# A hybrid encoder layer on eight cores: the transposes move from the matmul engine to DMA transposes on one queue

## The reference, cut to what matters

```python
def layer(x, c, S0, conv_prev, p):
    mod = (c @ w_mod + b_mod)[:, None, :]
    sh1, sc1, g1, sh2, sc2, g2 = jnp.split(mod, N_MOD, axis=-1)
    h = rmsnorm(x, norm1_g) * (1 + sc1) + sh1
    m, S_new, buf = token_mixer(h, S0, conv_prev, ...)
    x = x + g1 * m
    h = rmsnorm(x, norm2_g) * (1 + sc2) + sh2
    gt, upv = jnp.split(h @ w_ffn_in, 2, axis=-1)
    x = x + g2 * ((jax.nn.silu(gt) * upv) @ w_ffn_out)
    return x, S_new, buf

def token_mixer(h, S0, conv_prev, ...):
    q, k, v, g, a, cb, cc, ch, ga, gb = split(h @ w_in)      # D_MODEL 1024, IN_DIM 8208
    S_new, o = gla_recurrence(q, k, v, log_sigmoid(a @ w_alpha + b_alpha) / 16, S0)
    o = rmsnorm per head(o) * gla_norm_g * silu(g)
    y_a = o @ w_gla_out
    conv, new_buf = causal_conv(cc * ch, conv_prev, conv_w, conv_b)
    y_b = (cb * conv) @ w_conv_out
    return (sigmoid(ga) * y_a + sigmoid(gb) * y_b) @ w_o, S_new, new_buf
```

## Time and profile before

| | |
|---|---|
| median of 3 runs | 1441.21 us (1440.6 to 1496.53) |
| the profiled execution | 1442.98 us, span of its slowest core 1441.4 us (others 1428.5 to 1437.5) |
| mean granted TensorE clock | 0.969 to 0.979 |
| PE, DVE, ACT busy | 92%, 48%, 35% of the span |
| chain that ended last | 74% on PE |

### The profile page before, as it was taken

How to read it: one execution, slowest core, us unless ns; L and a number is a source line. 1 busy time by engine, 2 the same in 40 slices (tenths; PEclk the granted TensorE clock), 3 DMA queues, 4 the chain that set the end, 5 groups by cost and what they waited for, 6 DMA issues and landing times.

```text
span 1441.4 us, 22660 instructions; the slowest of 8 cores (1428.5 to 1441.4 us)
## 1 busy us (share of the span) xinstructions
PE 1333.1 (92%) x7660; PEld 695.5 (48%) x7660; DVE 688.4 (48%) x1257; ACT 504.3 (35%) x1122; POOL 109.8 (8%) x208
## 2 busy tenths in 40 slices
PE   1577999998989899889999999999999999999997
PEld 1333445444545455544445555555555445555443
DVE  1467557543656577642233334962122552212486
ACT  1576456432445455431211112981111001111233
POOL 3000100000000000011110120010000002000000
PEclk9778999998999999999999999999999999999999
DMA  9736401206211111154342366532223006222222
GB/s 173 212 117 154 52 9 30 52 2 59 51 23 23 23 23 23 23 96 73 52 74 38 62 102 135 179 68 37 40 35 44 1 1 103 36 40 35 59 103 110
DMA packets 42797, 92.66 MB, mean 64 GB/s; under 512 B 5206, under 2 KB 8166, under 8 KB 42684
## 3 DMA queue, kind: packets, MB, share of 16 engines
q0 software_dynamic: 29264, 53.02, 24.9%
q1 hardware_dynamic: 13420, 38.20, 8.2%
HBM read 133.95 MB, written 10.25 MB: 100 GB/s over the span
## 4 chain that ended last, share of the span: by engine, by line
PE 74%; ACT 9%; DMA 5%; DVE 5%; issue 5%; POOL 0%; ACTq 0%; DVEq 0%; SPq 0%; POOLq 0%
PE psum L464 72%; ACT sb_arena L447 6%; DMA sb_wring<-wfm 2%; DVE sb_arena L450 2%; PE psum L467 2%; ACT sb_tmpB L447 2%; DMA sb_wring<-w_in 1%; ACT sb_rstd L447 1%; DMA sb_wring<-w_mod 1%; DVE sb_arena L454 1%; DVE sb_arena L458 1%; DMA sb_arena<-xm 1%; DVE sb_tmpB L458 0%; POOL sb_wring L437 0%; DVE sb_arena L455 0%
## 5 line engine op out<-in xcount | busy, mean ns | idle before, releaser
L464 PE MATMUL psum<-sb_arena,sb_wring 128*128 128x384 bf16 (+3 forms) x4448 | 837.5, 347 | 11.5 <-DVE sb_arena L461 10.1
L464 PEld LDWEIGHTS psum<-sb_arena,sb_wring 128*128 128x128 bf16 x4448 | 430.1, 98 | 385.3 <-issue 44.2
L464 PE MATMUL psum<-sb_wring,sb_arena 128*128 128x512 bf16 (+2 forms) x1596 | 350.4, 378 | 4.3 <-DMA sb_wring<-w_in 4.3
L447 ACT ACTIVATE sb_tmpB<-psum 128x384 f32<-128x384 f32 (+1 forms) x264 | 139.6, 532 | 606.3 <-PE psum L464 576.1
L450 DVE TENSOR_TENSOR sb_arena<-psum,sb_tmpB 128x384 bf16<-128x384 f32 (+5 forms) x254 | 148.6, 587 | 324.6 <-PE psum L464 306.1
L464 PEld LDWEIGHTS psum<-sb_wring,sb_arena 128*128 128x128 bf16 (+1 forms) x1596 | 155.8, 99 | 184.0 <-issue 7.4
L437 POOL DMA_DIRECT2D sb_wring<-wfm x140 | 75.3, 545 | 912.5 <-PE psum L464 769.0
L450 DVE TENSOR_TENSOR sb_tmpB<-psum,sb_tmpB 128x384 f32<-128x384 f32 (+2 forms) x80 | 47.8, 598 | 171.0 <-PE psum L464 170.5
L450 DVE TENSOR_TENSOR sb_arena<-psum,sb_arena 128x512 f32<-128x512 f32 (+2 forms) x106 | 72.6, 685 | 35.3 <-PE psum L464 35.1
L447 ACT ACTIVATE sb_arena<-sb_arena 128x1024 bf16<-128x1024 f32 (+2 forms) x60 | 60.5, 1010 | 76.7 <-DVE sb_arena L450 61.8
L467 PE MATMUL psum<-sb_identb,sb_arena 128*128 128x128 bf16 (+2 forms) x636 | 58.4, 234 | 24.6 <-DVE sb_arena L454 22.1
(11 more groups left out here) (94 smaller groups left out, 582.3 us busy)
## 6 DMA issues: line engine op xcount, KB each, us to landing
sb_wring<-wfm POOLq DMA_DIRECT2D x140, 256.0 KB, 6.1
sb_arena<-xm SPq DMA_DIRECT2D x29, 512.0 KB, 5.5
sb_arena<-xp SPq DMA_DIRECT2D x16, 512.0 KB, 8.2
ym<-sb_arena SPq DMA_DIRECT2D x16, 512.0 KB, 2.7
sb_wring<-w_ffn_out POOLq DMA_DIRECT2D x22, 256.0 KB, 4.6
sb_wring<-w_in POOLq DMA_DIRECT2D x16, 256.0 KB, 9.7
sb_wring<-w_mod POOLq DMA_DIRECT2D x16, 256.0 KB, 7.8
sb_wring<-w_o POOLq DMA_DIRECT2D x8, 256.0 KB, 8.0
```

What stands on the lines that cost most here:

```text
L447: return P.op("act", lambda e: e.activation(out=out, in_=in_, func=func, **kw), reads=reads, writes=writes)
L464: return P.op("pe", lambda e: e.matmul(out, lhsT=lhsT, rhs=rhs, start=start, stop=stop), reads=reads, writes=writes)
```

## The change

Every transpose of rows (`norm_b`, `post`), of the recurrence's output (`gla_C`) and of the prefix keys (`pre_ktm`) becomes a DMA transpose issued by SP, SBUF to SBUF in bf16. The 600 PE transposes of these places go; 124 others stay. One DMA transpose takes a whole tile of 128 rows by 1024 features (33 tiles in the prelude, 17 in the recurrence, 17 in the output projection); the four of the keys take 128 by 2048. The result arrives unmodulated in its final place, and DVE modulates it there in place, 8 operations of up to 512 columns a block, where ACT and DVE shared this work before. In `wo_gen` the scaling of the rows moves from DVE to ACT. Row loads move from SP to POOL, except those of the first two blocks; the residual rows are loaded by POOL behind the weights of `w_o`, with the first two feed-forward weights among them. The first two prefix blocks are normed (and block 1 is loaded) ahead of `mod_fm_gen`; the load of block 1 waited for the twelfth weight before. The prelude's rounds are arranged anew, the fillers in `wo_gen` are five in place of two, the first two feed-forward tiles take the last group last, and the last `taps` of a convolution channel runs a step earlier.

```diff
-        for c_ in (1536, 512, 1024):
+        hTp, r_hTp, r_hTpr = [], [], []
+        for c_ in (0, 512, 1024, 1536):
...
+        def dmat(out, in_, reads, writes):
+
+            return P.op("sp", lambda e: e.dma_start_transpose(out=out, in_=in_), reads=reads, writes=writes, dma=True)
...
-                dma("sp", xin[xi][0:R, :], src, after, [r_xin[xi]])
+                dma("sp" if i < 2 else "pool", xin[xi][0:R, :], src, after, [r_xin[xi]])
...
+                if i < NPB:
+                    dmat(hTp[i % 4][:, :, j * 128:(j + 1) * 128], xnP[xo], [r_xnP[xo]], [r_hTpr[i % 4][j]])
+                else:
+                    t = GTILES[i - NPB][j]
+                    dmat(hT[:, :, t * 128:t * 128 + R], xnP[xo][0:R, :], [r_xnP[xo]], [r_hTr[t]])
...
+            for k in range(KT):
+                for (c, n, seq) in runs:
+                    v = dst[:, k, col0 + c:col0 + c + n]
+                    ts(v, v, modT[:, 1, k, seq:seq + 1], modT[:, 0, k, seq:seq + 1], ALU.mult, ALU.add, raws + [r_modT[1], r_modT[0]], [dregs[k]])
+                if k % 2 == 1:
+                    yield
...
         def pre_ktm(pb):
+
             st = pb % 2
-            for t in range(4):
-                ki = pb * 4 + t
-                b = newbank()
-                for h in range(NH):
-                    tr(psb(b)[:, h * 128:(h + 1) * 128], kdP[st][:, h, t * 128:(t + 1) * 128], identb[:, :], [r_kdP[st][h], r_identb], [r_ps[b]])
-                cp(kdtmP[ki], psb(b)[:, 0:512], [r_ps[b]], [r_kdtmP[ki]])
-                yield
+            dmat(kdtmP[pb].rearrange("p (a d) -> p a d", a=16), kdP[st].rearrange("p h t -> p (h t)"), r_kdP[st], [r_kdtmP[pb]])
...
-            bT = mbank()
-            for k in range(KT):
-                tr(psb(bT)[:, k * 128:k * 128 + R], ogb[oi][0:R, k * 128:(k + 1) * 128], identb[0:R, 0:R], [r_ogb[oi], r_identb], [r_ps[bT]])
-            cp(ogT[:, :, c0:c0 + R], psb(bT).rearrange("p (k r) -> p k r", k=KT)[:, :, 0:R], [r_ps[bT]], [r_og[t]])
+            dmat(ogT[:, :, c0:c0 + R], ogb[oi][0:R, :], [r_ogb[oi]], [r_og[t]])
...
-                    cx, r_cx = taps(g)
-                    yield
-                    cv(g, cx, r_cx)
+                    tp = taps(g)
                     if g == 3:
-                        cx, r_cx = taps(4)
+                        tp4 = taps(4)
+                    yield
+                    cv(g, *tp)
                     yield
-                cv(4, cx, r_cx)
+                cv(4, *tp4)
...
+                act(xv[xi][0:R, :], xres[0:R, t, :], AF.Copy, r_xres[t] + [r_rstd[gi]], [xg[xi]], scale=rstd[0:R, gi * 4:gi * 4 + 1])
+                dmat(h2T[:, :, c0:c0 + R], xv[xi][0:R, :], [xg[xi]], [r_h2r[t]])
...
+                if t in (8, 11, 14, 17, 18):
                     next(filler)
...
+                for g in range(NG):
+                    if t == min(GTILES[g][-1] + 3, 18):
+                        post(g)
...
+                order = [(j, g) for j in range(2) for g in range(NG - 1)] + [(0, NG - 1), (1, NG - 1)] + order[2 * NG:]
...
+        begin(1)
+        run(nas[1])
+        run(mod_fm_gen([(0, 0, 0), (1, 1, 1)]))
...
-        ldafter = [[mdregs[11]]]
-        begin(1)
         begin(2)
         run(norm_t(0))
...
+        begin(3)
+        spread([(pre_gate(0), 6), (norm_t(1), 4)])
         state = pre_state()
+        spread([(nas[2], 7), (pre_gate(1), 6), (pre_keys(0, wk), 4)])
+        pre_ktm(0)
         for s_ in range(0, NBK - 2):
 
             parts = []
-            begin(s_ + 3)
             begin(s_ + 4)
+            parts.append((chain(iter([None] * 2), norm_t(s_ + 2), iter([None] * 2)), 8))
...
+            kb = s_ + 1 if s_ == 0 else s_
+            if kb < NPB and s_ != 1:
+                parts.append((pre_keys(kb, wk), 4))
+            if 1 <= s_ < NPB - 1:
                 parts.append((pre_gate(s_ + 1), 6))
...
+            dma("pool", xres[0:R, t, :], x_src(t), [], r_xres[t])
+            if t == 5:
+                f1w[0] = (wfm("f1", 0), wfm("f1", 22))
```

More of the change, by code:

```diff
@@ L28 @@
 TM = 2112
-TX = 2114
+TX = 2128
 GRP = [(0, 512), (512, 384), (896, 384), (1280, 384), (1664, 448)]
@@ L268, in build, with raw_regs @@
         r_hTh = mreg("hTh", [(A0 + (k * TX + TM) * 2, A0 + (k * TX + TX) * 2) for k in range(KT)], "hT")
+        def raw_regs(name, off, width, cols, grp_):
+            return [mreg("%s_%d" % (name, i), [(off + (k * width + c0) * 2, off + (k * width + c0 + n) * 2) for k in range(KT)], grp_)
+                    for i, (c0, n) in enumerate(cols)]
+        r_hTr = raw_regs("hTr", A0, TX, CH, "hTr")
         xres = view(A0, 17 * 4096, F32).rearrange("p (n d) -> p n d", d=D)
@@ L284, in build @@
         r_h2 = fm_regs("h2", B0, KT, TM, GRP, "h2")
+        r_h2r = raw_regs("h2r", B0, TM, CH, "h2r")
         nfg = view(B0, 4096, F32)
```

127 lines of the change are left out of this document (47 added, 80 removed).

## The result

The changed kernel takes 1521.1 us, the kernel before 1441.0 us beside it on the same chip: 1.055 times as long, 95% interval 1.053 to 1.057. It is 5% slower where 3% faster was forecast. In some executions the cores of one die run at a lower clock (1626 and 1696 us here, 1497 before); the ratio leaves these out and the median does not, and by the ratio the loss is 78.7 us. The profiled core's span went from 1441.4 to 1516.6 us, 75 us more.

A forecast was written before the change was run, and what follows sets the result against it. PE, busy 92% of the span, was taken as the bound except where it waits. Prelude and start 22, recurrence 13 and output projection 7 made 42 us off the 1441.4 us span, for 1400 us; range 1370 to 1430.

The forecast's parts named there:

- 1 to 2 us a piece for the queue: Prelude: a 256 KB DMA transpose occupies the queue 1 to 2 us and lands after 2 to 3 us.
- The start, "+5": Start: loading block 1 wholly beside the weights PE waits for costs 5 us, between nothing and 11.6.
- first gate matmul later than 50 us: Start of the prelude: sign that the forecast is wrong, for the first gate matmul behind `mod_fm_gen`.
- 1.3 us in each of seven rounds: Prelude: DVE's exposed wait for a block's four transposes, 9 us in all.
- the queue rival: Prelude and output projection: transposes run one after another and limit the pace; at 6.1 us each, 1560 us; chance 0.12.
- 0.71 of the sum: Prelude, 42 to 160 us: same overlap of PE and ACT work afterwards, 85 us, 33 less; 36 with later transposes.
- the named 0.7: Prelude: a clock below 0.7 was a sign that the forecast is wrong.
- the rival's 0.5: Prelude: mean clock falls from 0.80 to 0.5 as PE idles more, eating the gain; 1421 us, chance 0.18.
- The recurrence, 13 us: Recurrence: 7.5 us of transposes, 4 of waits at channel heads and 1.5 of clock saved; between 7.5 and 19.
- The output projection, 7 us off: Output projection: 17 tiles fall from 3.96 to 3.54 us each, limited by DVE; 1.5 us with dearer modulations.
- 0.28 us a modulation: Output projection: DVE's price for modulating 384 columns, from an SBUF row; 0.40 by the PSUM row.
- The eight-fold price: Prelude and output projection: eight pieces of 1.31 us a tile, 10.5 us a tile, about 1796 us; chance 0.03.

The follow-up runs named there:

- e4: Changed kernel with squares, scaling and transposes of block 1 written behind the modulation vectors' matmuls; 1518.4 us.
- e10: e9 with row loads of blocks 0 and 1 first, then modulation vectors, then scaling and transposes of both blocks; 1482.6 us.
- e9: Changed kernel with row loads of each block held, by a bare dependence, until the transposes two blocks earlier have landed; 1486.8 us.
- e13: e10 with the next stage's weight loads held until the last prelude block's transposes have landed; 1474.4 us.
- e14: e13 with the modulation of a block moved to the end of its round; 1473.2 us.
- e1: Kernel before with only the recurrence's part of the change (output tiles by DMA transpose, earlier taps); 1431.3 us, ratio 0.993.
- e17: e1 with five 512 KB copies through GpSimd's queue beside each output tile, its transpose held until the first has landed; 1538.7 us.

## Why the prediction was wrong

The forecast span was 1399.4 us and the measured 1516.6, 117 us more: 89 of them lie ahead of `ss`, 3 in the recurrence, 27 in the output projection, and 2 go the other way elsewhere. The step that failed most is the price of a transpose, "1 to 2 us a piece for the queue", taken from a quiet row and used beside loads. There it was up to 13 us.

- **The start, "+5".** It was 29 us. I priced block 1's load as bytes beside the weights (2.1 MB), and did not follow the order on SP: the load is issued behind four transposes, which took 31 us beside the weights and were in no term of the start. "Squares and scaling of block 1 then lie in time in which ACT is idle, and cost nothing" failed too. What counts is not that ACT is idle but what waits behind that scaling on DVE: the evictions of `modT`, and by them PE's banks. That alone is the smaller part, as e4, which writes them ahead of it, is only 2 us faster; with the transposes behind the weights (e10) the first gate matmul is 12 us late in place of 29. The bound named as "first gate matmul later than 50 us" was crossed.
- **The prelude, "1 to 2 us a piece", "1.3 us in each of seven rounds".** The piece was taken from the 512 KB store in 2.7 us and held in quiet stretches (1.23 us, landing 2.7 us). Beside loads the last packet came after 8.1 us, and DVE waited 65 us in seven waits, 9 us each. e9 shows that 32 to 34 us of the time come from loads released together with the transposes, e13 that 10 come from the weights. The 72 modulations were 88, as the last group has 24; the 16 more are of 32 columns. The row that should have warned was the 0.56 share of the DMA engines, cited there only for the queue rival.
- **"0.71 of the sum".** Even with quick transposes (e14) the stretch is 24 us longer than before, where a gain of 36 was counted. Half of it is the start; the overlap was not the same afterwards, and no row had spoken for that. What paces these rounds (row loads, PE at a clock of 0.80, or the chain through the gate) the runs leave open.
- **The clock.** It fell to 0.74 from 42 to 160 us, to 0.68 from 75 to 235, just below the named 0.7; with quicker rounds it rose to 0.80 (e14). Its direction was right, and it did not reach the rival's 0.5. It falls after waits here; what it costs in the prelude was not measured apart. In the output projection it took back the 7.5 us of the transposes.
- **The recurrence, 13 us.** Right in mechanism, 9 to 10 us in size. The term that was too large is the waits at the head of a channel: 4 us and 1.5 for the clock were counted, and they went from 10.6 to 7.8 us, 3 less. With 7.5 us of transposes that makes up what was measured.
- **The output projection, 7 us off.** It was 19 to 20 on. 0.28 us a modulation was wrong: eight in a row take 3.79 us, 0.47 each, and the last group's are 24. But that is the smaller part (5 us without the prompt's); 10 come of residual loads in one burst beside the first transposes, which the sum did not hold.
- **The rivals.** "The queue is the limit" had the right side and, with transposes beside loads, the right place. It was priced as a constant time a piece, which made 1560 in the prelude and in the projection alike. The piece held SP for 1.2 us or for up to 13, by what was in flight. The eight-fold price is refuted: eight squares take 1.23 us in quiet.

## What to carry to other kernels

Before a PE transpose is moved to the DMA engines, look at what else these carry in that very stretch: it pays where they are quiet and its result is read late (e1, 9 us), and costs where loads run beside it and an in-order engine waits (the prelude lost 70 us, the output projection 19; keeping loads and weights away from the transposes gave back 48 and 10). If it must stand among loads, let them wait for its landing, with a bare dependence rather than a registered read, or write them behind it in its own queue. When a load or a norm is moved ahead, write out for each queue it passes what now stands behind it.

## What the runs showed of the hardware

- One transpose of 256 KB holds its queue for 1.22 to 1.25 us in quiet; the known landings are 2.7 us in the changed kernel's recurrence and 4.7 to 4.8 in e1. The eight squares in it are not priced one by one.
- Beside GpSimd's loads four of them held SP for 1.8, 12.3, 13.0 and 3.5 us (start) and 1.6, 11.0, 10.8 and 3.4 us (output projection), in packets of about 250 bytes against 2.2 KB of the weights. The first of a row of transposes holds the queue for little even then; those behind it wait.
- Beside copies in packets of 16 KB (e17) a transpose's last packet ended 11.9 us after its issue at the median, against 2.3 in e1, though the queue was held for 1.5 us only: a short issue does not tell of a quick landing.
- A modulation in place on DVE, bf16 to bf16 in SBUF, takes 0.41 us busy for 512 columns, 0.38 for 384 and 0.29 for 32, so most of it does not depend on the width; in a row of eight of 384 there are 0.47 us from one to the next. The eviction from PSUM takes 0.53 us for 512 columns.
